# VectorE's instruction order in the two Strassen feed-forward stages of a 1024-token, 22-matrix kernel

## The chip, the cores and the metric

One Trainium2 chip, one of its cores. The metric is device microseconds (us) of one execution of the whole kernel, lower is better. PE is TensorE, DVE is VectorE, ACT is ScalarE, POOL is GpSimd, SP is SyncE (it issues the loads).

## What is computed

Two blocks over a sequence of 1024 tokens, width 1024: two layers of mixed attention, and then one macaron block, which has a SwiGLU feed-forward before and after its mixer. The change touches the feed-forwards alone, which the reference has as

```python
def _swiglu(h, w_gu, w_down):
    g, u = jnp.split(h @ w_gu, 2, axis=-1)
    return (jax.nn.silu(g) * u) @ w_down

    for l in range(DEPTH_2):
        x = x + FFN_RES * _swiglu(_rmsnorm(x, norm_ffn1[l]), w_ffn1_gu[l], w_ffn1_down[l])
        ...
        x = x + FFN_RES * _swiglu(_rmsnorm(x, norm_ffn2[l]), w_ffn2_gu[l], w_ffn2_down[l])
```

with h 1024 x 1024, w_gu 1024 x 5632 (g and u 2816 columns each, 22 tiles of 128) and w_down 2816 x 1024. The root of the mean square is a factor per token: the kernel multiplies by the gain first, starts the matmuls on that, and puts the root (ROOT) on their results.

## The kernel before, in words

**Exact products from halves.** Every float32 operand is cut into a float16 part hi and a bfloat16 part lo, and one product is three matmuls (L1182 to L1184: hi*hi, hi*lo, lo*hi) of 128x128 by 128x512. hi is a copy to float16 by ACT and a clip to the largest float16 by DVE in place; lo = source - hi comes from POOL or from DVE.

**Where an order is written.** Each engine has its own program, written out by hand: the five programs run side by side, each strictly in its own order, and meet at semaphores alone. An instruction that waits holds up all that stands behind it on its engine. Nothing is scheduled by a planner.

**A feed-forward, `ffn(idx)`, idx 1 and 2** (they have the same code on each engine):

1. DVE adds seven tiles of squares (`add_squares`, into `stats`), PE sums them over the partitions, DVE scales that (`variance`, L2180, and with it gives back the accumulator that PE needs for the tile after it), ACT makes the reciprocal root, and `refine` does one Newton step (ROOT in `stats`).
2. The first PLAIN_F = 4 pairs of tiles of g and u are computed plainly, two pairs at a time in the four PSUM tiles. DVE's `plain_pair(f)` takes g times ROOT, lets ACT make the silu, takes u, multiplies by ROOT and cuts the result into its halves.
3. The other 18 pairs (`BLOCKS`) go by a Strassen-like scheme (Winograd's, 7 products in place of 8). The activation is cut into quarters Q11, Q12, Q21, Q22 (each 128 x 2048 in the tensor `residual`). Four differences of quarters are made in place by `term_sum`, each after the one before it; ACT copies T1, T3, T2 and T4 to float16 (`term_part`), DVE clips them, and DVE (T1, T3: `term_split`) or POOL (T2, T4: `term_rest`, L1071) makes the low halves. ACT's order is: silu of pair 0, first weight part, T1, T3, T2, silu of pair 1, weight parts.
4. The weights of a block come as one load of 1 MB (`panel_raw` or `ffn_extra`, by turns, issued when POOL is through with the block before). DVE makes four sums of quarters (`weight_sum(b, 0..3)`, in a chain), ACT makes seven float16 copies, DVE clips them (`weight_clip(b, 0..6)`), and POOL makes the seven low halves (`weight_rest`, L1066).
5. PE's `block(b)` then runs seven products of 12 matmuls each into four accumulators. Between them stand waits; those that matter here are

```python
                        if i == 3:
                            pe.wait_ge(evicted, 9 * n + 1)
                        if i == 5:
                            pe.wait_ge(evicted, 9 * n + 3)
```

   The fourth product (i = 3) waits for DVE's first eviction of the block, `evict(b, 0)`: U2 = second accumulator + the copy of the first, since it writes over the second accumulator. The sixth (i = 5) waits for evictions 1 and 2. `evict(b, 0)` itself waits for the second product and for ACT's copy of the first accumulator (`first_copy`), and in block 0 that copy waits for POOL's T4 (`term_ready_pool`), whose source it writes over.
6. `keep_block(b - 1)`: evictions 6, 7 and 8 of the block before, times ROOT, and its halves. DVE does this when the last product of block b - 1 is done, while PE runs products 1 to 3 of block b.

DVE's loop over the blocks before the change was, in each turn: `keep_block(b - 1)`, the four `weight_sum(b + 1, n)`, `evict(b, 0)`, three weight clips, `evict(b, 1)` and `evict(b, 2)`, two clips, `evict` 3 to 5, two clips. The helper `tt` (L2156) records every tensor_tensor of DVE, so one line stands for many kinds of work; the tensor names tell them apart.

Of the kernel before, what the change touches and what calls it, by code (L numbers as in the profile page):

```python
# [28 lines left out]
ALU = mybir.AluOpType  # L29
# [19 lines left out]
PLAIN_F = 4  # L49
# [336 lines left out]
def build(nc, io):  # L386
    ctx = ExitStack()
    with ctx:
# [84 lines left out]
        B_T1, B_T2, B_T3 = [parts(22528 + 2048 * c, 2048) for c in range(3)]  # L473
# [4 lines left out]
        Q11, Q12, Q21, Q22 = (X4[:, k:k + 4, c:c + HALF] for k in (0, 4) for c in (0, HALF))  # L478
# [120 lines left out]
        normed = sem("operand_normed")  # L599
# [1542 lines left out]
        def _(dve):  # L2142
# [12 lines left out]
            def tt(out, a, b, op):  # L2155
                return V_.tensor_tensor(out, a, b, op)  # L2156
# [21 lines left out]
            def variance(v, section, turn, t, n, eps):  # L2178

                V_.tensor_scalar(v, ready(section, turn, t)[:, :], 1.0 / n, eps, ALU.mult, ALU.add)\  # L2180
                  .then_inc(tile_taken[t % 4], 1)
# [162 lines left out]
            def add_squares(idx):  # L2344

                for k in range(1, KT):
                    dve.wait_ge(square_made, 8 * (idx - 1) + k + 1)
                    tt(SQSUM, SQT[0] if k == 1 else SQSUM, SQT[k], ALU.add).then_inc(square_added, 1)
                    dve.wait_ge(square_added, 7 * (idx - 1) + k)
# [207 lines left out]

            def ffn(idx):
                add_squares(idx)
                variance(SILP[0], f"rms{idx}", 0, 3, D, 1e-6)  # L2560
                refine(SILP[0], ROOT, AFP[0], 3 * LAYERS + 1 + (17 if idx == 2 else 0) + (idx == 2))
                restart()

                def plain_pair(f):
# [7 lines left out]
                    chained(tt(AFP[j], AFP[j], ROOT, ALU.mult))  # L2572
                    t = slice(f * T, (f + 1) * T)
                    split(AP_[0][:, t], AP_[1][:, t], AFP[j], act_split)

                def term_sum(out, a, b, n, after):
                    dve.wait_ge(normed, 12 * (idx - 1) + after)
                    tt(out, a, b, ALU.subtract).then_inc(normed, 1)

                def term_clip(home, n):  # L2580
                    dve.wait_ge(term_hi, 4 * (idx - 1) + n)
                    return V_.tensor_scalar(home[0], home[0], HI_MAX, -HI_MAX, ALU.min, ALU.max)

                def term_split(home, q, n):
                    hi, lo = [v.rearrange("p (k t) -> p k t", k=4) for v in home]
                    chained(term_clip(home, n))
                    tt(lo, q, hi, ALU.subtract).then_inc(term_ready, 1)

                def weight_sum(b, n):
                    a11, a12, a21, a22 = raw_block(b)  # L2590
                    s1, s2, s4 = sums_of(b)
                    g = block_of(idx, b)
                    if n == 0:
                        dve.wait_ge(raw_loaded[b % 2], 16 * ((BLOCKS - b % 2 + 1) // 2 * (idx - 1) + b // 2 + 1))
                        if b > 0:
                            dve.wait_ge(weight_lo, 7 * (g - 1) + 6)
                    out, x, y, op = ((s1, a21, a22, ALU.add), (s2, s1, a11, ALU.subtract), (a21, a11, a21, ALU.subtract),
                                     (s4, a12, s2, ALU.subtract))[n]
                    tt(out, x, y, op).then_inc(sum_made, 1)
                    if n in (0, 1):  # L2600
                        dve.wait_ge(sum_made, 4 * g + n + 1)
# [48 lines left out]
                    split(AP_[0][:, t], AP_[1][:, t], FACT, act_split)  # L2650

                plain_pair(0)
                term_sum(Q11, Q12, Q11, 9, 8)
                term_sum(Q12, Q22, Q12, 10, 9)
                term_sum(Q22, Q22, Q11, 11, 10)
                term_sum(Q21, Q21, Q22, 12, 11)
                plain_pair(1)
                for n in range(4):
                    weight_sum(0, n)
                term_split(B_T1, Q11, 1)  # L2660
                term_clip(B_T2, 3).then_inc(term_clipped, 1)
                term_split(B_T3, Q12, 2)
                for i in range(5):
                    weight_clip(0, i)
                for f in range(2, PLAIN_F):
                    plain_pair(f)
                for i in range(5, 7):
                    weight_clip(0, i)
                term_clip(B_T4, 4).then_inc(term_clipped, 1)
                for b in range(BLOCKS):  # L2670
                    more = b + 1 < BLOCKS
                    if b > 0:
                        keep_block(b - 1)
                    if more:
                        for n in range(4):
                            weight_sum(b + 1, n)
                    evict(b, 0)
                    if more:
                        weight_clip(b + 1, 0)
                        weight_clip(b + 1, 1)  # L2680
                        weight_clip(b + 1, 2)
                    evict(b, 1)
                    evict(b, 2)
                    if more:
                        weight_clip(b + 1, 3)
                        weight_clip(b + 1, 4)
                    for step in (3, 4, 5):
                        evict(b, step)
                    if more:
                        weight_clip(b + 1, 5)  # L2690
                        weight_clip(b + 1, 6)
# [438 lines left out]
```

## Time and profile before

| | |
|---|---|
| time, median of 3 runs | 3399.25 us (3399.2 to 3400.58) |
| the profiled execution | 3400.38 us, of which the span from first to last instruction is 3398.6 us |
| busy: PE, DVE, POOL, ACT | 3241.8 us (95%), 1831.8 (54%), 1611.1 (47%), 1131.2 (33%) |
| chain of waits that ended last | PE 83%, DVE 11%, issue 3%, ACT 2%, POOL 1% |
| granted TensorE clock, mean | 0.989 |
| first product of block 0 on PE | starts at 1227.41 us in the first, at 2807.17 us in the second feed-forward |

Busy time of PE counts the pipelined length of its matmuls, so a short wait hardly lowers it; waits are better read from the view of waits and from the timeline. The chain gives, for each moment, the engine that the end hung on. A row of a timeline is: start in us from the span's start, duration in us, engine, line, operation, out<-in, shapes, count, and in brackets the idle time of the engine before it with what ended it.

### The profile page before, as it was taken

Reading aid. Unit: us, or ns where it says so; the run is one execution under the profiler, and the core shown is the slowest. Engines: PE = TensorE matmul, PEld = TensorE weight load, DVE = VectorE, ACT = ScalarE, POOL = GpSimd, SP = SyncE. Lnnn points to the kernel's source line nnn. Section 1 sums busy time; section 2 is a strip of 40 time slices with the busy share of each in tenths; the row PEclk is TensorE's granted clock in tenths of the full one; section 3 lists DMA queues with packets and bytes.
Section 4 is the critical chain, followed back from the end, with each engine's and each line's share of the span. In section 5 each row is a group of like instructions: output and inputs, shape, how many; then the busy total and the mean of one; then the engine's idle time right before and its main releaser. Section 6 shows DMA issues by size and latency. Waiting matters only on the chain.

```text
span 3398.6 us, 47704 instructions
## 1 busy us (share of the span) xinstructions
PE 3241.8 (95%) x18771; PEld 1657.2 (49%) x19068; DVE 1831.8 (54%) x3065; ACT 1131.2 (33%) x2104; POOL 1611.1 (47%) x1100
## 2 busy tenths in 40 slices
PE   8999998999999879999999999999999998999999
PEld 4555653655654334444445554555554443444444
DVE  4365558146547876664113366666666687676200
ACT  1434422234332522221002445555554432222000
POOL 4555752455664244443333566655664434444332
PEclk9999999999999989999999999999999998999999
DMA  3122112112121211112222011111112211111212
GB/s 131 40 51 62 58 56 101 38 50 65 38 80 39 88 49 51 61 50 96 70 70 90 29 58 52 50 51 52 51 36 93 84 63 50 50 62 38 103 50 83
DMA packets 59276, 211.71 MB, mean 62 GB/s; under 512 B 7344, under 2 KB 7728, under 8 KB 58544
## 3 DMA queue, kind: packets, MB, share of 16 engines
q1 hardware_dynamic: 54304, 191.34, 17.3%
q10 hardware_dynamic: 4752, 17.30, 1.3%
q8 instruction: 154, 2.52, 0.3%
q14 instruction: 66, 0.54, 0.1%
HBM read 181.36 MB, written 20.97 MB: 60 GB/s over the span
## 4 chain that ended last, share of the span: by engine, by line
PE 83%; DVE 11%; issue 3%; ACT 2%; POOL 1%; DMA 0%; DVEq 0%; SPq 0%; POOLq 0%; ACTq 0%
PE pair L1184 24%; PE pair L1182 23%; PE pair L1183 21%; DVE residual L2156 5%; PE pair L1402 3%; PE pair L1371 3%; DVE arena L2156 3%; PE pair L1383 2%; PE pair L1620 1%; PE pair L1646 1%; PE pair L1631 1%; DVE arena L2167 1%; PE pair L1574 1%; PE pair L1202 1%; DVE pair L2156 1%
## 5 line engine op out<-in xcount | busy, mean ns | idle before, releaser
L1182 PE MATMUL pair<-operand,panel_parts 128*128 128x512 f16 x1808 | 691.4, 382 | 42.0 <-DVE operand L2156 26.2
L1184 PE MATMUL pair<-operand,panel_parts 128*128 128x512 f16 x1808 | 689.0, 381 | 8.5
L966 POOL TENSOR_SCALAR panel_parts<-panel_raw 128x1024 f16<-128x1024 f32 (+3 forms) x204 | 208.7, 1023 | 918.7 <-issue 645.0
L1183 PE MATMUL pair<-operand,panel_parts 128*128 128x512 bf16 x1648 | 628.6, 381 | 0.0
L1182 PE MATMUL pair<-arena,panel_parts 128*128 128x512 f16 (+1 forms) x1248 | 470.5, 377 | 16.3 <-DVE residual L2156 7.5
L967 POOL TENSOR_TENSOR panel_parts<-panel_raw,panel_parts 128x1024 bf16<-128x1024 f32 (+3 forms) x204 | 472.6, 2317 | 17.0
L1184 PE MATMUL pair<-arena,panel_parts 128*128 128x512 f16 (+1 forms) x1248 | 469.5, 376 | 4.6
L1003 POOL TENSOR_SCALAR arena<-arena,row_inv 128x256 f32<-128x256 f32 (+7 forms) x256 | 347.5, 1370 | 237.7 <-DVE row_inv L2222 237.5
L1183 PE MATMUL pair<-arena,panel_parts 128*128 128x512 bf16 (+2 forms) x1160 | 436.3, 376 | 0.0
L1182 PEld LDWEIGHTS pair<-operand,panel_parts 128*128 128x128 f16 x1808 | 177.5, 98 | 275.7 <-issue 94.8
L2159 DVE SCALAR_TENSOR_TENSOR residual<-pair,residual 128x1024 f32<-128x1024 f32 (+1 forms) x64 | 61.3, 958 | 420.9 <-PE pair L1184 392.4
L1184 PEld LDWEIGHTS pair<-operand,panel_parts 128*128 128x128 bf16 x1808 | 177.6, 98 | 216.3 <-issue 5.0
L1137 POOL TENSOR_SCALAR arena<-arena,row_inv 128x384 f32<-128x384 f32 (+1 forms) x128 | 192.0, 1511 | 157.8 <-DVE row_inv L2839 157.8
L1183 PEld LDWEIGHTS pair<-operand,panel_parts 128*128 128x128 f16 x1808 | 177.8, 98 | 177.9 <-issue 8.8
L1833 ACT ACTIVATE arena<-arena,neg_max 128x256 f32<-128x256 f32 (+7 forms) x256 | 156.0, 611 | 322.1 <-DVE neg_max L2203 321.6
L2203 DVE CUSTOM_DVE_ANT_0 arena<-pair,arena 128x256 f32<-128x256 f32 (+7 forms) x256 | 133.8, 559 | 146.5 <-PE pair L1371 79.7
L2156 DVE TENSOR_TENSOR arena<-arena 128x1024 f32<-128x1024 f32 (+3 forms) x143 | 195.8, 1369 | 22.3 <-ACT arena L2063 10.6
L1182 PEld LDWEIGHTS pair<-arena,panel_parts 128*128 128x128 f16 x1248 | 121.8, 98 | 175.2 <-issue 41.1
L1184 PEld LDWEIGHTS pair<-arena,panel_parts 128*128 128x128 bf16 x1248 | 122.0, 98 | 144.1 <-issue 0.3
L1183 PEld LDWEIGHTS pair<-arena,panel_parts 128*128 128x128 f16 x1248 | 122.1, 98 | 131.5 <-issue 3.5
L2156 DVE TENSOR_TENSOR residual<-pair,residual 128x512 f32<-128x512 f32 (+1 forms) x168 | 116.8, 713 | 125.8 <-PE pair L1184 124.4
L1735 ACT ACTIVATE arena<-pair 128x512 f32<-128x512 f32 (+2 forms) x210 | 99.4, 504 | 156.8 <-PE pair L1184 128.5
(300 smaller groups left out, 5797.2 us busy)
## 6 DMA issues: line engine op xcount, KB each, us to landing
panel_raw<-in_wl SPq DMA_DIRECT2D x58, 512.0 KB, 3.5
panel_raw<-in_wm SPq DMA_DIRECT2D x56, 512.0 KB, 3.6
ffn_extra<-in_wgu SPq DMA_DIRECT2D x18, 1024.0 KB, 5.0
panel_raw<-in_wgu SPq DMA_DIRECT2D x18, 1024.0 KB, 5.2
panel_raw<-in_wdn SPq DMA_DIRECT2D x32, 512.0 KB, 3.5
residual<-residual_spill SPq DMA_DIRECT2D x31, 512.0 KB, 6.4
residual_spill<-residual ACTq DMA_DIRECT2D x24, 512.0 KB, 2.6
panel_raw<-in_wgu SPq DMA_DIRECT2D x16, 512.0 KB, 3.7
```

The costliest lines, as they stand in the source:

```text
L966: chained(nc.gpsimd.tensor_scalar(hi[:, c], RAW[:, s, c], HI_MAX, -HI_MAX, ALU.min, ALU.max))
L967: nc.gpsimd.tensor_tensor(lo[:, c], RAW[:, s, c], hi[:, c], ALU.subtract).then_inc(panel_split[s], 1)
L1003: nc.gpsimd.tensor_scalar(p, p, RI[:, b:b + 1], None, ALU.mult).then_inc(slot_scaled, 1)
L1137: nc.gpsimd.tensor_scalar(p, p, RI[:, b:b + 1], None, ALU.mult).then_inc(mix_scaled, 1)
L1182: nc.tensor.matmul(out, stat[0], mov[0], start=first, stop=False, skip_group_check=skip)
L1183: nc.tensor.matmul(out, stat[0], mov[1], start=False, stop=False, skip_group_check=skip)
L1184: return nc.tensor.matmul(out, stat[1], mov[0], start=False, stop=last, skip_group_check=skip)
L1371: m = nc.tensor.matmul(out[:, c:c + w], q_of(s, u), k_of(s, u)[:, c:c + w], start=True, stop=True)
L1402: m = nc.tensor.matmul(OUTL[u.h * HD:(u.h + 1) * HD, (i // 2) * P:(i // 2 + 1) * P], v_of(s, u, kt), PTL[g][:, c0:c0 + P], start=j == 0, s ...
L1833: nc.scalar.activation(p, p, ACT.Exp, bias=NM[:, b:b + 1], scale=-1.0, accum_out=RS[:, b:b + 1]).then_inc(slot_probs, 1)
L2156: return V_.tensor_tensor(out, a, b, op)
L2203: m = V_.tensor_tensor_reduce(out=probs_of(n, s, u), in0=score_cols(s, u), in1=bias_of(s, u), scale=-1.0, scalar=3e38, op0=ALU.add, op1=AL ...
```

## The change

Only DVE's program is touched, in both feed-forwards:

- two of the four differences of quarters (Q11 and Q12) are moved from behind `plain_pair(0)` to ahead of `variance`;
- the clip of T2 is put ahead of the cut of T1; the cut of T3 is moved from ahead of the five weight clips and `plain_pair(2)` to between `plain_pair(2)` and `plain_pair(3)`;
- in the loop over the blocks `evict(b, 0)` is put ahead of the four weight sums of the next block.

No instruction is added or taken away, and none changes its shape.

```diff
@@ -2557,6 +2557,12 @@
             def ffn(idx):
                 add_squares(idx)
+                def term_sum(out, a, b, n, after):
+                    dve.wait_ge(normed, 12 * (idx - 1) + after)
+                    tt(out, a, b, ALU.subtract).then_inc(normed, 1)
+
+                term_sum(Q11, Q12, Q11, 9, 8)
+                term_sum(Q12, Q22, Q12, 10, 9)
                 variance(SILP[0], f"rms{idx}", 0, 3, D, 1e-6)
@@ -2650,20 +2652,18 @@
                 plain_pair(0)
-                term_sum(Q11, Q12, Q11, 9, 8)
-                term_sum(Q12, Q22, Q12, 10, 9)
                 term_sum(Q22, Q22, Q11, 11, 10)
                 term_sum(Q21, Q21, Q22, 12, 11)
                 plain_pair(1)
                 for n in range(4):
                     weight_sum(0, n)
+                term_clip(B_T2, 3).then_inc(term_clipped, 1)
                 term_split(B_T1, Q11, 1)
-                term_clip(B_T2, 3).then_inc(term_clipped, 1)
-                term_split(B_T3, Q12, 2)
                 for i in range(5):
                     weight_clip(0, i)
-                for f in range(2, PLAIN_F):
-                    plain_pair(f)
+                plain_pair(2)
+                term_split(B_T3, Q12, 2)
+                plain_pair(3)
                 for i in range(5, 7):
                     weight_clip(0, i)
@@ -2671,11 +2671,10 @@
                     if b > 0:
                         keep_block(b - 1)
+                    evict(b, 0)
                     if more:
                         for n in range(4):
                             weight_sum(b + 1, n)
-                    evict(b, 0)
-                    if more:
                         weight_clip(b + 1, 0)
```

On VectorE, at the start of a feed-forward: the seven adds of squares, the scaling L2180 that PE and ACT wait for, and the first Newton instruction. Of the difference between the two orders:

```order
 L2156 TENSOR_TENSOR stats<-stats,arena 128x1024 x4
 L2156 TENSOR_TENSOR stats<-stats,ffn_extra 128x1024 x2
+L2156 TENSOR_TENSOR residual<-residual 128x4x512 x2
 L2180 TENSOR_SCALAR arena<-pair 128x1024
 L2156 TENSOR_TENSOR arena<-stats 128x1024
```

Two of the differences of quarters (`residual<-residual`) now stand ahead of L2180; the other two stay behind the first plain pair.

On VectorE, where block 0 begins, before the change: the two clips of weight parts 5 and 6, the clip of T4 (`operand<-operand`), the four weight sums of block 1, and then `evict(0, 0)` (`residual<-pair,residual`):

```order
L2606 TENSOR_SCALAR panel_parts<-panel_parts 128x512 x2
L2582 TENSOR_SCALAR operand<-operand 128x2048
L2156 TENSOR_TENSOR arena<-panel_raw 128x512
L2156 TENSOR_TENSOR arena<-arena,panel_raw 128x512
L2156 TENSOR_TENSOR panel_raw<-panel_raw 128x512
L2156 TENSOR_TENSOR arena<-panel_raw,arena 128x512
L2156 TENSOR_TENSOR residual<-pair,residual 128x512
```

and with it:

```order
L2608 TENSOR_SCALAR panel_parts<-panel_parts 128x512 x2
L2584 TENSOR_SCALAR operand<-operand 128x2048
L2156 TENSOR_TENSOR residual<-pair,residual 128x512
L2156 TENSOR_TENSOR arena<-panel_raw 128x512
L2156 TENSOR_TENSOR arena<-arena,panel_raw 128x512
L2156 TENSOR_TENSOR panel_raw<-panel_raw 128x512
L2156 TENSOR_TENSOR arena<-panel_raw,arena 128x512
```

The eviction has gone past four sums; the same exchange stands in every later block but the last, behind `keep_block`.

## Rows read from the trace of the kernel before

**Rows 1.** View of waits, first feed-forward (1120 to 1640 us): total, times, longest
```profile
PE pair L1182 <- DVE residual L2156: 25.1, 17, 10.0
PE pair L1182 <- DVE arena L2156: 5.8, 1, 5.8
```
**Rows 2.** View of waits, second feed-forward (2700 to 3230 us)
```profile
PE pair L1182 <- DVE residual L2156: 24.8, 17, 9.7
```
**Rows 3.** Timeline of PE, end of third and start of fourth product of one block
```profile
1363.74 0.38 PE L1184 MATMUL pair<-arena,panel_parts 128*128 128x512 f16 x1
1365.07 0.38 PE L1182 MATMUL pair<-arena,panel_parts 128*128 128x512 f16 x1 [0.94 <-DVE residual L2156]
1365.28 0.38 PE L1183 MATMUL pair<-arena,panel_parts 128*128 128x512 bf16 x1
```
**Rows 4.** Timeline of DVE, same block: first sum, evict 0, three clips, evict 1
```profile
1361.58 0.68 DVE L2156 TENSOR_TENSOR residual<-panel_raw 128x512 f32<-128x512 f32 x1
...
1364.23 0.68 DVE L2156 TENSOR_TENSOR residual<-pair,residual 128x512 f32<-128x512 f32 x1
1364.84 0.69 DVE L2606 TENSOR_SCALAR residual<-residual 128x512 f16<-128x512 f16 x3
1367.85 0.69 DVE L2156 TENSOR_TENSOR residual<-pair,residual 128x512 f32<-128x512 f32 x1 [2.33 <-PE pair L1184]
```
**Rows 5.** Timelines of ACT (first copy) and POOL (first low half), same block
```profile
1358.98 0.60 ACT L1735 ACTIVATE residual<-pair 128x512 f32<-128x512 f32 x1 [3.09 <-PE pair L1184]
...
1365.20 1.34 POOL L1066 TENSOR_TENSOR residual<-panel_raw,residual 128x512 bf16<-128x512 f32 x1 [7.42 <-DVE residual L2606]
```
**Rows 6.** Timelines of DVE and POOL around the first feed-forward's root
```profile
1163.29 1.22 DVE L2156 TENSOR_TENSOR stats<-stats,ffn_extra 128x1024 f32<-128x1024 f32 x1
1168.31 1.23 DVE L2180 TENSOR_SCALAR arena<-pair 128x1024 f32<-128x1024 f32 x1 [3.79 <-PE pair L1202]
1188.63 2.29 DVE L2156 TENSOR_TENSOR residual<-residual 128x2048 f32<-128x2048 f32 x1
1190.96 3.01 DVE L2156 TENSOR_TENSOR residual<-residual 128x2048 f32<-128x2048 f32 x1
...
1166.67 1.04 POOL L966 TENSOR_SCALAR panel_parts<-panel_raw 128x1024 f16<-128x1024 f32 x1 [5.75 <-PE pair L1184]
```
**Rows 7.** Timelines of ACT and DVE: first weight part, and pair 1's u
```profile
1192.65 0.63 ACT L1735 ACTIVATE ffn_extra<-ffn_extra 128x512 f16<-128x512 f32 x1 [15.80 <-DMA ffn_extra<-in_wgu]
...
1200.08 1.22 DVE L2156 TENSOR_TENSOR arena<-pair,arena 128x1024 f32<-128x1024 f32 x1 [4.98 <-ACT arena L1924]
```
**Rows 8.** Timelines where block 0 begins: DVE first sum and evict 0, POOL T4, ACT copy
```profile
1239.22 1.63 DVE L2156 TENSOR_TENSOR arena<-panel_raw 128x512 f32<-128x512 f32 x1
...
1246.56 0.69 DVE L2156 TENSOR_TENSOR residual<-pair,residual 128x512 f32<-128x512 f32 x1
...
1240.27 4.50 POOL L1071 TENSOR_TENSOR operand<-residual,operand 128x2048 bf16<-128x2048 f32 x1
...
1244.88 0.60 ACT L1735 ACTIVATE residual<-pair 128x512 f32<-128x512 f32 x1 [9.30 <-POOL operand L1071]
```
**Rows 9.** Windows: us, busy of PE, PEld, DVE, ACT, POOL, granted clock, DMA share, GB/s
```profile
1241.00:1252.00 11.00, 4.61 (x11) 1.65 (x12) 6.81 (x7) 3.19 (x6) 7.32 (x4) 0.54 0.28 95
```
**Rows 10.** Timelines of DVE and POOL around the second feed-forward's root
```profile
2742.32 1.22 DVE L2156 TENSOR_TENSOR stats<-stats,ffn_extra 128x1024 f32<-128x1024 f32 x1
2748.07 1.22 DVE L2180 TENSOR_SCALAR arena<-pair 128x1024 f32<-128x1024 f32 x1 [4.52 <-PE pair L1202]
...
2746.43 1.04 POOL L966 TENSOR_SCALAR panel_parts<-panel_raw 128x1024 f16<-128x1024 f32 x1 [5.22 <-PE pair L1184]
2747.55 2.12 POOL L967 TENSOR_TENSOR panel_parts<-panel_raw,panel_parts 128x1024 bf16<-128x1024 f32 x1
...
2762.17 4.05 POOL L967 TENSOR_TENSOR panel_parts<-panel_raw,panel_parts 128x1024 bf16<-128x1024 f32 x1
```
**Rows 11.** Timeline of DVE, the five weight clips of block 0
```profile
1219.73 3.98 DVE L2606 TENSOR_SCALAR ffn_extra<-ffn_extra 128x512 f16<-128x512 f16 x5
```

More of the change, by code:

```diff
@@ L2574, in plain_pair @@
                     split(AP_[0][:, t], AP_[1][:, t], AFP[j], act_split)
-                def term_sum(out, a, b, n, after):
-                    dve.wait_ge(normed, 12 * (idx - 1) + after)
-                    tt(out, a, b, ALU.subtract).then_inc(normed, 1)
                 def term_clip(home, n):
```

## The prediction, made before the change was run

> **What bounds the kernel now.** The page comes first: PE is busy for 95% of the span and the chain runs through it for 83%, but 11% of the chain is DVE. So there are places where PE stands and DVE is what it stands for. The view of waits of the two feed-forwards names them. In the first, PE's L1182 waited 17 times for DVE's `residual`, 25.1 us, the longest 10.0, and once for `arena`, 5.8 us [rows 1]; in the second it is the same, 24.8 and 9.7 [rows 2]. The longest is block 0. The other 16 make 15.1 us, 0.94 each, and they are blocks 1 to 16 (block 17 has no next block, so no sums stand ahead of its eviction).
>
> The timeline of one such block shows what is behind it. The last matmul of product 3 starts at 1363.74, the first of product 4 at 1365.07, 1.33 us later, where matmuls otherwise follow at 0.21 [rows 3]. So the stall is 1.12 us (the idle time in the row is less, since a matmul's row is longer than its pitch). PE was released by evict 0, which ran from 1364.23 to 1364.91. Ahead of it on DVE stood the four weight sums, from 1361.58 [rows 4]. Their results are wanted for the next block. ACT's copy of the first accumulator, the other thing evict 0 needs, was there at 1359.58 [rows 5].
>
> **Part 1, evict 0 ahead of the sums (blocks 1 to 16).** It can start where the first sum did, at 1361.58. The second product is done by then: with product 4 due at 1363.95 (1363.74 + 0.21) and 12 matmuls of 0.215 to a product, product 3 began at 1361.4, and a matmul's row ends 0.17 after the next one's start. Evict 0 ends at 1362.26 and PE is released 0.16 later, as it was before (1364.91 to 1365.07). Product 4 is due at 1363.95, so 1.5 us are left and the stall goes wholly: 16 x 1.12 x 2 = 35.8 us.
>
> What is late next? The sums start 0.7 later, but evict 0 no longer stands between them and the clips, so the first clip stays at 1364.84 and POOL at 1365.20 [rows 4, 5]. ACT's copies of the sums come 0.7 later and are off the path: these weights are wanted a whole block later. Evict 1 may start 1.12 earlier, at 1366.73, and DVE is through with the three clips at 1365.53. Evicts 1 and 2 take 1.4 and must end before product 6, due at 1363.95 + 2 x 2.58 = 1369.1; that gives evict 1 until 1367.5, 2.0 us after DVE is free. All later evictions hang on PE's products. The next load of weights waits for POOL's low halves, which keep their place against PE. DVE has room: it was idle for 2.33 us before evict 1 alone [rows 4], and a block of 84 matmuls takes PE 18.1 us in place of 19.2. Cost beside the gain: nothing, while those 2.0 us hold.
>
> **Part 2, evict(0, 0).** It gains less than its place suggests. It needs ACT's first copy, which waited for POOL's T4 until 1244.88 [rows 8]. DVE will now stand at the eviction and the sums behind it wait. What goes is the remainder of the sums: the copy ends at 1245.48, evict 0 can start at about 1245.6 instead of 1246.56, 1.0 us. POOL's 4.50 [rows 8] also gets shorter: DVE's first sum, 1.63 where such a sum takes 0.68 [rows 4], ended at 1240.85, after POOL's operation began at 1240.27; if POOL waited for it, 0.5 us more goes. Bounds 1.0 and 1.5; I take 1.5, since the sum's extra length shows that the two do exclude each other. Twice: -3.0 us. Block 1's sums now end at about 1248.4 instead of 1246.7, ten us before their block begins. The granted clock is 0.54 around this start [rows 9], as PE has stood for 10 us, and it will have stood at least as long: no change taken; if the half-rate stretch moved by one or two us it would be worth about 1 us either way.
>
> **Part 3, T2's clip, T3 and the plain pairs.** T3's cut no longer delays `plain_pair(2)`, so product 1 starts some 3 us earlier and the 5.8 us wait [rows 1] shrinks. It is worth nothing: PE then waits the longer before product 4, whose release (part 2) hangs on `plain_pair(3)` and the clips behind it, and ahead of those stands the same work as before. T3 is ready before product 4, since it stands one plain pair ahead. Cover gone: if part 2's wait were not there, this would show.
>
> **Part 4, two differences ahead of the root.** DVE is idle for 3.79 us before L2180 [rows 6]. Free, such a difference takes 2.29, against POOL 3.01 [rows 6]. In the first feed-forward Q11 runs from 1164.55 to 1166.85; then POOL has just begun an operation (1166.67), which is when I take the difference of 3.01 and not that of 2.29, so Q12 ends at 1169.88. L2180 starts at 1169.8 instead of 1168.31: 1.5 us late, and with it PE's next tile, the panels that follow on POOL, and the weight load behind them on SP's queue. That load releases ACT at 1192.65 [rows 7], ACT makes three copies and pair 1's silu, and DVE waits 4.98 us for that at 1200.08 [rows 7]. So all 1.5 us arrive, and what the two sums leave free behind plain pair 0 falls into that idle time: +1.5.
>
> In the second feed-forward the adds end at 2743.54 and Q12 would run from 2745.9 to 2748.2. POOL's operation comes at 2746.43 [rows 10], after Q12's start. If Q12 is then undisturbed, L2180 starts at 2748.1 instead of 2748.07, no delay; with the 3.01 of the other row it would be 0.8 late. I take none, since the difference at 1188.63 [rows 6] took its 2.29 with the next operations of both engines close behind it. The Trainium skill ("SBUF — State Buffer", section "Who interferes with whom") says that whichever of the two starts first holds the shared port for its whole instruction and the other blocks; by it this term is 0.0, by the contended row alone +0.8. POOL's second operation then falls on `refine` (some 0.8 us on DVE alone, not on PE). At 2762.17 POOL's low half took 4.05 where a free one takes 2.12 [rows 10], for it stood behind a difference; with two of them gone and DVE's order shifted by 0.8 it waits less, and the weight load goes out earlier by between 0 and 1.9. I take 1.4: DVE's cut of pair 0 then still costs POOL part of it. It comes through the same chain as above: -1.4.
>
> **Sum.** -35.8 - 3.0 + 1.5 - 1.4 = -38.7. The profiled execution took 3400.38 (span 3398.6), which gives 3361.7. It lies 1.1 above the median of the runs, 3399.25, so the expected median is **3361**, between the two (1.1% faster). Changes below 0.2%, 6.8 us, cannot be told from none here.
>
> **The rivals.**
>
> *POOL holds DVE up and the stall comes back at product 6 (slower).* The place: the sums and three clips between evict 0 and evict 1. Five such clips took 3.98 us against POOL, where three take 0.69 free [rows 11, 4], and a sum took 1.63 in place of 0.68 [rows 8, 4]. If all were contended, DVE would be free at 1364.84 + 4 x 0.95 + 3 x 1.25 = 1372.4 and evict 1 start 4.9 us after its latest moment of 1367.5. Each block then loses 4.9 and wins 1.12: 32 x 3.8 = +121, less the 2.9 of the other parts, 3518. With the clips alone it is 1.1, and nothing changes: about 3396. It decides from 1368.8 on: 1.3 too late makes it slower by over 0.2%. Against it: POOL was idle for 7.42 us until 1365.20 [rows 5], as it is fed by these very clips. The same page's rule, that the second to issue waits for the whole instruction, would give these numbers if POOL were at work there; the trace has it idle. 2 in 100.
>
> *Another releaser.* The releaser is inferred from semaphores; if product 4 hung on a weight part or T term too, the change would do nothing: 3396 to 3402. Against it: the stall is the same 1.12 in sixteen blocks, 0.16 after evict 0. 3 in 100.
>
> *Half a gain.* Evict 0 stands at its inputs' very moment; if something on DVE or ACT then moves the later evictions so that about half the stall returns at product 5 or 6: -18 in place of -35.8, 3379. For it speaks only that the new loop has never run at 18.1 us a block. 7 in 100.
>
> *The root comes later than I take.* If all four moved differences take 3.01, L2180 is 2.3 late in the first (1164.55 + 6.05 = 1170.6) and 1.5 late in the second feed-forward, and the 1.4 is not won: +3.8 in place of +0.1, 3364. If PE's next tile then also begins at half rate, some 2 us more each, 3368. 10 in 100 for both.
>
> The forecast itself: 78 in 100. Its own bounds: part 2 and 4 reach from -2.0 + 1.5 + 0.8 = +0.3 to -3.0 + 0.7 - 1.9 = -4.2 (Q12 of the first undisturbed), and 2 us for the clock, so 3358 to 3366. The range takes in the late root and part of the half gain at the top: 3356 to 3372, which leaves about 15 in 100 out. Faster by over 0.2%: 0.95; within 0.2%: 0.03; slower: 0.02.
>
> **What would show it.** Right: in the view of waits PE's waits for `residual` fall from 17 to 1 in each feed-forward, fourth products follow third ones at 0.21 us, and blocks repeat at 18.1 instead of 19.2 us. DVE's evict 0 directly follows `keep_block`. The wait before product 1 drops to 2 to 4 us, the one before product 4 of block 0 grows and stays ended by DVE's `residual`. L2180 comes 1.5 us later after its adds in the first feed-forward and at the same time in the second. Wrong: any repeated wait of PE at product 5 or 6, a POOL operation between evict 0 and evict 1, or a block period over 18.3 us.

## The result, and the profile after

The changed kernel takes 3362.02 us (median of 4 runs, 3360.74 to 3364.86) against 3399.68 (3399.2 to 3400.58, 4 runs): a ratio of 0.989, 95% interval 0.9873 to 0.9907. The profiled execution took 3360.86, with a span of 3359.1. The prediction was 3361, from 3356 to 3372.

The page's part on the chain, where DVE had 11% before:

```profile
PE 90%; DVE 5%; issue 2%; ACT 2%; POOL 1%; DMA 1%; DVEq 0%; SPq 0%; ACTq 0%; POOLq 0%
```

The view of waits of the changed kernel, first feed-forward (1120 to 1640 us), answers to [rows 1]:

```profile
PE pair L1182 <- DVE residual L2156: 11.8, 1, 11.8
PE pair L1182 <- DVE arena L2156: 3.1, 1, 3.1
```

and the second (2700 to 3230 us) to [rows 2]:

```profile
PE pair L1182 <- DVE residual L2156: 13.5, 1, 13.5
PE pair L1182 <- DVE arena L2156: 1.5, 1, 1.5
```

Seventeen waits for `residual` have become one in each, block 0's. That one has grown. Counted from the end of the adds of squares, product 1 starts 0.3 us later than before in the first feed-forward and product 4 1.7 later; in the second they start 4.3 and 2.9 earlier. The timeline of PE at one of the later blocks, where product 4 begins:

```profile
1359.65 0.38 PE L1184 MATMUL pair<-arena,panel_parts 128*128 128x512 f16 x1
1359.87 0.38 PE L1182 MATMUL pair<-arena,panel_parts 128*128 128x512 f16 x1
```

The 1.33 us of [rows 3] are 0.22. The timeline of DVE in the same block, from evict 0 over the first sum and the three clips to evict 1, answers to [rows 4]:

```profile
1357.55 0.69 DVE L2156 TENSOR_TENSOR residual<-pair,residual 128x512 f32<-128x512 f32 x1
1358.16 0.68 DVE L2156 TENSOR_TENSOR residual<-panel_raw 128x512 f32<-128x512 f32 x1
...
1360.81 1.67 DVE L2608 TENSOR_SCALAR residual<-residual 128x512 f16<-128x512 f16 x3
1362.66 0.69 DVE L2156 TENSOR_TENSOR residual<-pair,residual 128x512 f32<-128x512 f32 x1 [0.18 <-PE pair L1184]
```

Evict 0 ends at 1358.24 and product 4 starts at 1359.87 without waiting. The three clips take 1.67 where they took 0.69, as the third of them now waits for POOL's low half (POOL's timeline):

```profile
1361.17 1.15 POOL L1066 TENSOR_TENSOR residual<-panel_raw,residual 128x512 bf16<-128x512 f32 x1 [7.49 <-DVE residual L2608]
```

The same low half took 1.34 before and delayed no clip [rows 4, 5]. That holds for every block that has a next one: before, POOL's operation took the longer time in all 34 places, and with the change the clip took it, 1.26 in place of 0.28, in 31 of 34.

All 17 steps from block to block, taken at each block's evict 3, are 18.13 us in both feed-forwards; before, 16 of them were 19.23.

**Where the 39.5 us of span went.** Each stretch between two marks of DVE's timeline, in the two profiled executions:

| stretch | before | after | difference | predicted |
|---|---|---|---|---|
| start to end of the first adds of squares | 1164.52 | 1164.78 | +0.3 | 0 |
| first feed-forward: to evict(0, 0) | 82.04 | 83.71 | +1.7 | 0.0 |
| to evict 3 of block 0 | 8.49 | 7.98 | -0.5 | 0 |
| to evict 3 of block 17 | 325.85 | 308.21 | -17.6 | -17.9 |
| to the end of the second adds of squares | 1162.65 | 1161.04 | -1.6 | 0 |
| second feed-forward: to evict(0, 0) | 82.77 | 79.86 | -2.9 | -2.9 |
| to evict 3 of block 0 | 8.79 | 7.68 | -1.1 | 0 |
| to evict 3 of block 17 | 325.86 | 308.21 | -17.7 | -17.9 |
| to the end | 237.61 | 237.60 | 0.0 | 0 |

The blocks carry 35.3 of it. What the first feed-forward lost ahead of block 0 (1.7) and what came back in three stretches that were forecast unchanged (0.5, 1.6, 1.1) is mostly TensorE's clock and the two early differences, which the next rows show. From evict(0, 0) to evict 3 of block 0 the granted clock was 0.68 before and 0.72 after in the first feed-forward, and 0.65 and 0.75 in the second.

**The start of the first feed-forward.** Timelines of DVE, and of POOL, at the root of the changed kernel, to be read against [rows 6]:

```profile
1164.81 5.33 DVE L2156 TENSOR_TENSOR residual<-residual 128x2048 f32<-128x2048 f32 x2
1170.07 1.21 DVE L2180 TENSOR_SCALAR arena<-pair 128x1024 f32<-128x1024 f32 x1
...
1183.57 2.71 POOL L966 TENSOR_SCALAR panel_parts<-panel_raw 128x1024 f16<-128x1024 f32 x1 [11.44 <-issue]
```

The two differences took 5.33 (2.29 and 3.01), and L2180 came 5.29 after the adds where it came 3.79 after them: 1.5 late, as forecast. But PE, released by it, then ran at about half rate. Windows of 1170 to 1174 us (columns as in [rows 9]), first before, then after:

```profile
1170.00:1174.00 4.00, 4.00 (x20) 1.83 (x19) 3.28 (x3) 1.90 (x2) 0.00 (x0) 1.00 0.45 131
```

```profile
1170.00:1174.00 4.00, 2.66 (x7) 1.01 (x8) 2.84 (x4) 2.34 (x2) 2.13 (x1) 0.63 0.17 39
```

The granted clock was 1.00 after an idle PE of about 1.4 us, and 0.63 now, after 2.9 us: part of these 4 us went at the lower of its two levels, 1.2 GHz in place of 2.4. From 1171.34 to 1174.30 matmuls follow at 0.43 us instead of 0.215, which makes PE's tile end 1.5 us later still. POOL's next operation, which began 15.8 us after the adds before, began at 18.8, took 2.71 in place of 2.01 as it met a remaining difference, and its second half (4.05 in both) ended 3.7 us later. The weight load behind it released ACT at

```profile
1196.67 0.63 ACT L1735 ACTIVATE ffn_extra<-ffn_extra 128x512 f16<-128x512 f32 x1 [18.07 <-DMA ffn_extra<-in_wgu]
```

31.9 us after the adds, against 28.1 [rows 7].

The lower clock does not follow from the idle time alone. Seven of the traced kernels have the early differences in the first feed-forward, and in all of them L2180 comes 5.29 us after the adds and PE idles for 2.9 us. In four (this one, the old order of T1 to T3, the relaxed wait and the turned-round start) PE restarts at the lower level. In three (the rest without evict 0, three sums ahead, two operations more) it restarts at full clock, and ACT is released 29.6 to 29.7 us after the adds, which is 1.5 us late and no more. The window of the kernel with two operations more, whose adds end within 0.01 us of the same place:

```profile
1170.00:1174.00 4.00, 2.65 (x13) 1.24 (x14) 2.84 (x4) 2.34 (x2) 2.15 (x1) 1.00 0.21 34
```

**The second feed-forward** went as worked out: POOL's operation came after the second difference had begun and was the one to wait, 2.67 in place of 1.04 [rows 10], and L2180 was not delayed. Timelines of DVE and POOL:

```profile
2725.76 4.62 DVE L2156 TENSOR_TENSOR residual<-residual 128x2048 f32<-128x2048 f32 x2
2730.29 1.22 DVE L2180 TENSOR_SCALAR arena<-pair 128x1024 f32<-128x1024 f32 x1
...
2728.60 2.67 POOL L966 TENSOR_SCALAR panel_parts<-panel_raw 128x1024 f16<-128x1024 f32 x1 [5.22 <-PE pair L1184]
2743.84 2.98 POOL L967 TENSOR_TENSOR panel_parts<-panel_raw,panel_parts 128x1024 bf16<-128x1024 f32 x1
```

POOL's low half took 2.98 in place of the 4.05 of [rows 10], and evict(0, 0) came 2.91 us earlier.

**Block 0.** Timelines of POOL, ACT and DVE, against [rows 8]:

```profile
1243.70 4.05 POOL L1071 TENSOR_TENSOR operand<-residual,operand 128x2048 bf16<-128x2048 f32 x1
...
1247.86 0.60 ACT L1735 ACTIVATE residual<-pair 128x512 f32<-128x512 f32 x1 [8.85 <-POOL operand L1071]
...
1248.49 0.69 DVE L2156 TENSOR_TENSOR residual<-pair,residual 128x512 f32<-128x512 f32 x1 [5.76 <-ACT residual L1735]
```

DVE stands at the eviction for 5.76 us, and POOL's T4 takes 4.05 instead of 4.50 as no sum is in its way.

**Between the feed-forwards** nothing was changed, yet 1.6 us went. There is a stretch at the end of the mixer where PE has stood and restarts at half rate; it was longer in the profiled execution before than in the one after. Eight of the twelve traces have 1162.6 to 1162.7 us for the whole stretch, so the 1161.04 of this one is the exception, and the gain of 1.6 belongs to the execution, not to the change. Windows, before and after:

```profile
2702.00:2710.00 8.00, 6.49 (x17) 2.36 (x18) 6.72 (x5) 4.41 (x5) 4.82 (x3) 0.57 0.85 316
```

```profile
2686.00:2694.00 8.00, 6.72 (x25) 2.73 (x26) 6.52 (x6) 4.18 (x5) 4.60 (x3) 0.79 0.87 320
```

### The profile page after: what moved, and what is told of

Read it like the earlier page. It is cut to its first block, busy times and chain, and to the rows that moved or that the text cites. A ratio compares the mean times of both kernels' runs of the same rounds, so it can differ in the third digit from the quotient of the medians.

```text
span 3359.1 us, 47704 instructions
## 1 busy us (share of the span) xinstructions
PE 3231.6 (96%) x18771; PEld 1658.5 (49%) x19068; DVE 1871.2 (56%) x3065; ACT 1130.5 (34%) x2104; POOL 1596.1 (48%) x1100
## 4 chain that ended last, share of the span: by engine, by line
PE 90%; DVE 5%; issue 2%; ACT 2%; POOL 1%; DMA 1%; DVEq 0%; SPq 0%; ACTq 0%; POOLq 0%
PE pair L1184 26%; PE pair L1182 26%; PE pair L1183 23%; PE pair L1402 3%; PE pair L1371 3%; PE pair L1383 2%; DVE arena L2156 2%; PE pair L1620 1%; PE pair L1646 1%; PE pair L1631 1%; PE pair L1574 1%; DVE stats L2156 1%; PE pair L1202 1%; DVE residual L2156 1%; PE pair L1360 0%
```

## The experiments

Every kernel was timed against the kernel before on the same chip; the kernel before had a median of 3398.86 beside the runs of evict 0 alone, the rest without it, the early differences taken back and the old order of T1 to T3; of 3399.48 beside the next four; and of 3400.68 beside the two with early differences in the second feed-forward only. Theory A is the prediction's: the repeated stall is the sums ahead of evict 0, and all else is small. Its rivals say that the start moves share in the gain, or that something else releases PE.

The stretch ahead of the first feed-forward took 1159.8 to 1166.6 us in the twelve traces, with the same code in all of them. So where a difference of a few us matters, the length of each feed-forward in the traces is given too, from the end of its adds of squares to evict 3 of block 17: 416.4 and 417.4 us before, 399.9 and 395.8 with the whole change.

### Evict 0 alone

The kernel before, with only this edit:

```diff
                         keep_block(b - 1)
+                    evict(b, 0)
                     if more:
                         for n in range(4):
                             weight_sum(b + 1, n)
-                    evict(b, 0)
```

> The kernel before with one edit: evict(b, 0) ahead of the four weight sums; sums, clips and splits at the start stay where they were. If the sums ahead of the eviction are the whole of the repeated stall, blocks repeat at 18.13 us and 32 x 1.10 = 35.2 us go, and evict(0, 0) gains its 1.5 us in each feed-forward too (3.0), so about 3361 to 3362, the same as the whole change within 2 us. Rival: the gain needs the earlier differences and splits as well (for instance because the first blocks would start late and stay late); then a good part is missing, 3375 or more, or the block period lies above 18.13.

3362.48 us (3361.15 to 3363.25), ratio 0.9893 (0.9876 to 0.9909). All 17 block steps are 18.13 us, and evict(0, 0) comes 80.5 us after the adds in the first feed-forward (before 82.0) and 81.0 in the second (82.8). The feed-forwards take 397.6 and 397.6 us, together 0.5 less than with the whole change. One exchange carries the whole gain.

### The rest without it

The whole change, with evict 0 put back behind the sums.

> The whole change with evict(b, 0) put back behind the four weight sums; the two early differences and the new order of clips and splits stay. If they are worth what the two traces suggest (the first feed-forward 1.7 us later, the second 1.4 us earlier), the time is within 3 us of 3399.7, and blocks repeat at 19.23 us. Rival: the start is where part of the 38 us came from: 3392 or less.

3400.5 us (3392.57 to 3403.61, 10 runs), ratio 1.0005 (0.9995 to 1.0015): no difference. The view of waits of its first feed-forward has the seventeen waits again:

```profile
PE pair L1182 <- DVE residual L2156: 30.0, 17, 15.0
```

Its profiled execution happened to be its fastest, 3392.57; 4.6 of its 7.8 us less had gone before the first feed-forward began, where the programs are the same. A single execution of it can't be used for a few us.

### The early differences taken back

```diff
                 add_squares(idx)
-                term_sum(Q11, Q12, Q11, 9, 8)
-                term_sum(Q12, Q22, Q12, 10, 9)
                 variance(SILP[0], f"rms{idx}", 0, 3, D, 1e-6)
...
                 plain_pair(0)
+                term_sum(Q11, Q12, Q11, 9, 8)
+                term_sum(Q12, Q22, Q12, 10, 9)
                 term_sum(Q22, Q22, Q11, 11, 10)
```

> The whole change with the two differences of quarters put back behind the first plain pair. In the first feed-forward L2180 follows the end of the adds by 3.8 us again and no longer by 5.3, PE's next tile does not fall to half rate, and evict(0, 0) comes 1.7 to 3 us earlier against the end of the adds; in the second L2180 stays at 4.5 us and evict(0, 0) comes 1.4 later. Together 0 to -2 us against the whole change: 3359 to 3363. Rival: the early differences pay in both, because they use DVE's idle time: then 3364 or more.

3361.48 us (3361.22 to 3363.67). Evict(0, 0) comes 80.5 us after the adds in the first feed-forward, where the whole change has 83.7, and 81.0 in the second, where it has 79.9. So in these traces the early differences cost 3.2 us in the one and win 1.2 in the other; over the whole feed-forwards (397.7 and 397.7) it is 2.2 and 1.9, and the times show no difference clear of the noise. The granted clock at PE's restart is full again (window of 1169 to 1174 us):

```profile
1169.00:1174.00 5.00, 4.96 (x23) 2.27 (x24) 3.69 (x4) 2.34 (x2) 0.36 (x1) 1.00 0.36 105
```

### Early differences in the second feed-forward only

```diff
                 add_squares(idx)
-                term_sum(Q11, Q12, Q11, 9, 8)
-                term_sum(Q12, Q22, Q12, 10, 9)
+                if idx == 2:
+                    term_sum(Q11, Q12, Q11, 9, 8)
+                    term_sum(Q12, Q22, Q12, 10, 9)
```

(and behind plain pair 0 for idx 1).

> The whole change, with the two early differences in the second feed-forward only; in the first they stand behind plain pair 0 as before. Against the end of the adds evict(0, 0) came 83.7 us later with them in the first and 80.5 without, and 79.9 with and 81.0 without in the second. So each is at its better value: about 3 us less than the whole change, 3358 to 3361. Rival: the difference in the first feed-forward is the clock's doing in one execution and averages out: 3361 to 3363.

3359.78 us (3358.02 to 3361.49), beside 3400.68 for the kernel before. Evict(0, 0) comes 80.5 and 79.6 us after the adds, the better value in each. The ranges of this kernel and of the whole change touch, so as a time the 2 to 3 us are likely and not settled. The feed-forwards of its trace take 397.7 and 395.3, together 2.7 less than those of the whole change.

### The old order of T1, T2 and T3

The whole change with

```diff
-                term_clip(B_T2, 3).then_inc(term_clipped, 1)
                 term_split(B_T1, Q11, 1)
+                term_clip(B_T2, 3).then_inc(term_clipped, 1)
+                term_split(B_T3, Q12, 2)
                 for i in range(5):
                     weight_clip(0, i)
                 plain_pair(2)
-                term_split(B_T3, Q12, 2)
                 plain_pair(3)
```

> The whole change with the old order of T1, T2 and T3 (T3's cut ahead of the five weight clips and the third plain pair). PE's wait before product 1 of block 0 grows by about 3 us in each feed-forward (3.5 to 6.4 between starts in the first, 1.8 to 4.8 in the second) and its wait before product 4 shrinks by as much; the time stays within 2 us of 3362. Rival: the 3 us arrive at the end, twice: 3368.

3362.76 us (3360.93 to 3365.34). In the first feed-forward's waits, PE's before product 1 is 6.2 us instead of 3.1, and the one before product 4 is 8.2 instead of 11.8:

```profile
PE pair L1182 <- DVE residual L2156: 8.2, 1, 8.2
PE pair L1182 <- DVE arena L2156: 6.2, 1, 6.2
```

The earlier third plain pair is paid back in full one wait later, as the prediction's part 3 has it.

### How much slack evict 0 has

The whole change, with evict 0 behind three of the four sums.

```diff
-                    evict(b, 0)
                     if more:
-                        for n in range(4):
+                        for n in range(3):
                             weight_sum(b + 1, n)
+                    evict(b, 0)
+                    if more:
+                        weight_sum(b + 1, 3)
```

> The whole change, but evict(b, 0) stands behind three of the four weight sums instead of ahead of all. In the changed kernel it ends 1.5 us before product 4 is due; three sums take 2.05 us. If that slack is real, 0.55 to 0.6 us per block come back, blocks repeat at 18.7 us, and 32 of them make +18, about 3380. Rival: the stall hangs on something else that the move happened to relieve (POOL's or ACT's order), then the period stays 18.13, or goes to 19.23 at once.

3375.6 us (3375.5 to 3375.78), ratio 0.9928 (0.9912 to 0.9945). The block steps are 18.63 us, so 0.50 came back in each of 32 blocks. The timeline of PE where product 4 starts, and of DVE with evict 0 between the third and the fourth sum:

```profile
1284.88 0.38 PE L1184 MATMUL pair<-arena,ffn_extra 128*128 128x512 f16 x1
1285.60 0.38 PE L1182 MATMUL pair<-arena,ffn_extra 128*128 128x512 f16 x1 [0.34 <-DVE residual L2156]
```

```profile
1284.77 0.68 DVE L2156 TENSOR_TENSOR residual<-pair,residual 128x512 f32<-128x512 f32 x1
1285.37 0.68 DVE L2156 TENSOR_TENSOR arena<-panel_raw,arena 128x512 f32<-128x512 f32 x1
```

PE starts 0.15 us after evict 0's end, at whatever place the end is, so the release is evict 0, and nothing else: the rival of another releaser is out. The time came out 4 us below the expected 3380; 2 of them are in the 32 blocks, which gave back 15.9 in place of 18.

### POOL's work between evict 0 and evict 1

The whole change, with two operations more per block. Their results go nowhere.

```diff
                         weight_clip(b + 1, 2)
+                        for _ in range(2):
+                            tt(STAT[:, _ * HALF:(_ + 1) * HALF], ROOT[:, 0:HALF], ROOT[:, HALF:T], ALU.add)
                     evict(b, 1)
```

> The whole change with two operations more on VectorE in each block, between the three weight clips and evict(b, 1): sums of two halves of ROOT into the unused first quarter of stats, 128x512, both inputs in SBUF, as a weight sum; 0.69 us each when free. The output does not depend on them. In the changed kernel evict 1 starts at 1362.66 and product 6 would be held from 1363.46 on; DVE is free at 1362.48. If POOL, which works there, holds each of them up for one of its 1.16 us operations, evict 1 starts near 1365.7, 2.2 late, and 32 blocks give +70, about 3433. If POOL and VectorE do not exclude each other, it starts at 1363.8, 0.3 late, +10, about 3372. If product 6 does not hang on evict 1 and 2 at all, 3362.

3422.67 us (3420.61 to 3427.99), ratio 1.0071 (1.0054 to 1.0088): 61 us more than the whole change, for 2 x 0.69 us of work in each of 34 places. The timeline of DVE in one block, and the one of POOL over the same time:

```profile
1291.00 3.20 DVE L2156 TENSOR_TENSOR stats<-stats 128x512 f32<-128x512 f32 x2
1294.13 0.68 DVE L2156 TENSOR_TENSOR residual<-pair,residual 128x512 f32<-128x512 f32 x1
```

```profile
1290.90 2.76 POOL L1066 TENSOR_TENSOR residual<-arena,residual 128x512 bf16<-128x512 f32 x2
```

The two sums take 3.20 in place of 1.4, 1.64 each: POOL and DVE go by turns. Product 6 then waits for evict 2, 17 times, 25.2 us in all:

```profile
PE pair L1182 <- DVE pair L2156: 25.2, 17, 1.9
```

The block steps are 19.18 or 20.16 us, so a block loses 1.05 or 2.03, where 2.2 were expected; 24 of the 34 steps are of the longer kind, 8 of the shorter, and two lose 0.04 or less. So the rival that would have made the change slower is a real mechanism, and the price was of the right size. What kept it away is that the changed kernel has only the third clip in POOL's way. With two operations more there, the loss is larger than what the change had won.

### The wait of block 0's first copy

The quarter that ACT's copy writes over is Q12, and evict 0 writes over a part of Q22; POOL's T4 reads Q21, which evict 1 is the first to write over. So the wait of the first copy for T4 does not protect the source of T4, as the description of the kernel before has it: the copy never touches that quarter.

```diff
                     if b == 0:
                         act.wait_ge(term_ready, 2 * idx)
-                        act.wait_ge(term_ready_pool, 2 * idx)
+                        act.wait_ge(term_ready_pool, 2 * idx - 1)
...
                     elif step == 1:
                         dve.wait_ge(product_done, 7 * g + 4)
+                        if b == 0:
+                            dve.wait_ge(term_ready_pool, 2 * idx)
```

> The whole change, where ACT's copy of the first accumulator of block 0 waits for T1, T2 and T3 alone, and evict(0, 1), which writes over Q21, waits for POOL's T4 instead. If POOL's T4 is what holds block 0's fourth product, evict(0, 0) follows T4's clip directly, some 5.8 us earlier in each feed-forward (6.0 instead of about 11.8 us idle before product 4), of which product 6 gives back 1 to 3, as evict(0, 1) then comes behind sums that wait for POOL: 3350 to 3356. Rival: block 0 is held by its chain on VectorE (plain pair 3 and the clips), and POOL's T4 lies in its shadow: 3360 or more.

3354.66 us (3350.08 to 3360.96), ratio 0.9862 (0.9846 to 0.9879). PE's wait before product 4 is 5.9 us in place of 11.8, and a new one of 3.0 stands before product 6, whose evictions come behind sums that POOL holds up:

```profile
PE pair L1182 <- DVE residual L2156: 5.9, 1, 5.9
PE pair L1182 <- DVE arena L2156: 3.0, 1, 3.0
PE pair L1182 <- DVE pair L2156: 3.0, 1, 3.0
```

So POOL's T4 did hold block 0, and half or more of what its removal frees is given back behind it: the feed-forwards take 398.3 and 392.1 us, 1.6 and 3.6 less than with the whole change. Its executions lie 11 us apart and the profiled one is the slowest: in it the stretches that the edit does not touch were 5.1 us longer than in the trace of the whole change. So the 7 us between the medians are uncertain by some us, and the traces show 5.

### Block 0 turned round

The relaxed wait, and T4, the first copy and evictions 0 to 2 of block 0 moved forward. DVE's part is below. On ACT T4's copy and the first copy go ahead of plain pair 3's silu, and on POOL T4 ahead of the low halves of weights 5 and 6. The loop then leaves out evictions 0 to 2 of block 0.

```diff
                 term_split(B_T3, Q12, 2)
+                term_clip(B_T4, 4).then_inc(term_clipped, 1)
+                evict(0, 0)
                 plain_pair(3)
                 for i in range(5, 7):
                     weight_clip(0, i)
-                term_clip(B_T4, 4).then_inc(term_clipped, 1)
+                evict(0, 1)
+                evict(0, 2)
```

> As the run with the relaxed wait, and in block 0 the order is turned round on three engines: T4 is copied, clipped and cut ahead of plain pair 3 (on POOL ahead of the low halves of weights 5 and 6), the first copy and evict(0, 0) stand ahead of plain pair 3 too, and evicts 1 and 2 of block 0 ahead of block 1's sums. Then product 4 follows product 3 without a wait, product 6 waits for evict 2 behind plain pair 3 (about 1244.4 in the first feed-forward), and product 7 starts at about 1247 where it starts at 1258.6 now: 10 to 12 us in each feed-forward, 3338 to 3345. Rival: the work on VectorE is the same, so block 0's end hangs on its sum and the wait only moves to product 6, 7 or the first product of block 1: 3352 or more.

3341.43 us (3341.13 to 3348.93), ratio 0.9835 (0.9819 to 0.9852). Product 4 follows product 3 without a wait. What PE still waits for from 1150 to 1300 us is product 1, the root, block 1's fourth product and product 6, in the order of the lines:

```profile
PE pair L1184 <- DVE arena L2160: 3.0, 1, 3.0
PE pair L1184 <- DVE arena L2184: 2.9, 1, 2.9
PE pair L1184 <- DVE residual L2160: 2.7, 1, 2.7
PE pair L1184 <- DVE pair L2160: 1.7, 1, 1.7
```

(The added lines move the helpers' numbers: L2160 is `tt`, L2184 the scaling.) This kernel has the lowest median of the study, 20.6 us under the whole change, and is by 1.65% faster than the kernel before. Its feed-forwards take 392.1 and 386.7 us, 7.8 and 9.1 less than with the whole change and not 10 to 12; the other 3.3 us of the difference between the two traced spans lie in stretches that the edit does not touch.

### Both together

The turned-round start, with early differences in the second feed-forward only.

> The turned-round start of block 0 (the run called hoisted) together with early differences in the second feed-forward only. The first plain tiles and the weight load come some 1.5 to 3 us earlier in the first feed-forward, and with block 0 now close behind them that arrives at the end: 3337 to 3341 against 3341.4. Rival: block 0 now hangs on the time at which PE ends the plain tiles and not on the load; then 1 us or less is gained.

3342.88 us (3341.85 to 3344.98), ratio 0.9832 (0.9818 to 0.9845). As a time it is not faster than the one before it, and the expected gain is missed. The traces show why this does not speak for the rival. Evict(0, 0) comes 67.1 us after the first adds in place of 70.1, and the first feed-forward takes 389.0 us in place of 392.1, so the 3.1 us do arrive at its end; the second takes 387.1 in place of 386.7. But the stretch ahead of the first feed-forward, which has the same code, took 1165.26 us in this profiled execution and 1159.82 in the other. A gain of 3 us is lost among such differences between executions.

## Why the prediction was right

**Part 1, the sums ahead of evict 0: right.** 32 x 1.12 = 35.8 was forecast and 35.3 measured (17.64 and 17.65 between evictions 3 of blocks 0 and 17); the edit alone gives the whole gain. The slack of 1.5 us was right: evict 0 ended 1.63 before product 4 started, 0.15 of which is the release, and three sums ahead brought back 0.50. **The slack of evict 1 was half of what I wrote.** The prediction left the three clips at 0.69 and had 2.0 us. POOL's low half caught the third clip (1.67), DVE was free at 1362.48 and evict 1 had until about 1363.46. It cost nothing, but two operations more took the rest, as their run shows. A sign of being wrong was badly chosen here: "a POOL operation between evict 0 and evict 1" occurs with the change (1361.17), and it stood there before it as well (1365.20, between 1364.23 and 1367.85 [rows 4, 5]), so it could not tell anything.

**Part 2, evict(0, 0): right.** 1.5 us in each feed-forward were forecast; with evict 0 alone it came 1.5 earlier after the adds in the first and 1.8 in the second. Of the two bounds the upper was the right one, since POOL's T4 went from 4.50 to 4.05.

**Part 3, T3 and the plain pairs: right.** The old order gives the same time with the waits shared out otherwise; product 1 starts 3.2 us later with it in the first feed-forward and 2.6 in the second. The wait before product 1 was forecast at 2 to 4 us and is 3.1 in the first and 1.5 in the second.

**Part 4, the early differences: right in the second, mis-sized in the first.** Forecast +1.5 and -1.4, measured up to evict(0, 0) by the trace without them +3.2 and -1.2. The 1.5 us by which L2180 is late was exact. The step that failed is that all behind it was taken to keep its distance: PE, idle for 2.9 us in place of 1.4, restarted at the lower clock, its tile took 1.5 us longer, and POOL's panel met a difference at another point. Where the clock stayed up, the forecast holds: with two operations more, whose program is the same up to that point, evict(0, 0) comes 82.0 us after the adds, 1.5 later than the 80.5 without early differences. So the term is 1.5 or about 3.2, as the clock falls, and the prediction had the clock only in a rival, for both feed-forwards; it fell in the first alone.

**The total was right also by luck.** 1.7 too few in the first feed-forward's start were made up by shorter stretches at half rate elsewhere (0.5, 1.1 and the 1.6 in the mixer), which no step forecast. The changed kernel's own executions differ by 4 us, and those of the change without evict 0 by 11.

**A size in a rival.** The bound of 1.3 us, from which the rival of POOL makes the kernel slower by 0.2%, leaves out the 2.9 us of the other parts; with them it is 1.4.

The Trainium skill's rule ("SBUF — State Buffer", section "Who interferes with whom"), that the later of VectorE and GpSimd waits for the other's whole instruction, was the one to go by. By it Q12 in the second feed-forward would run free, and it did (4.62 for two). It also fits the two added operations at 1.64 each, between POOL operations of 1.16 free. Of the 1.64 some 0.95 are the wait. What the rule does not give is who comes first when both are ready at the same moment: the third clip is recorded 0.04 us after POOL's low half before the change and with it, and the clip waits in none of the 34 places before and in 31 of them with it.

The rival of half a gain and the one of another releaser did not occur: no wait repeats, and PE's release follows evict 0 wherever it is put.

## What to carry to other kernels

In a hand-written order, put the instruction that the busiest engine waits for ahead of work that is only wanted a stage later, and first look up in the trace that its other inputs are there at that moment; the gain is the stall, not the length of what it overtakes. Then work out the slack of the next release too, with the shared port counted in: here 1 us was left, and two operations more of 0.69 us each turned the gain into a loss. Work moved into an engine's idle time ahead of a release is free only if it ends in time: it was 1.5 us late, and cost 1.5 us where the waiting engine's clock held and 3.2 where it fell.

## What was not expected of the hardware

After an idle PE of 2.9 us, before one and the same tile, the granted clock was at its lower level for some 3 us in four traces (0.63 from 1170 to 1174 us in the changed kernel) and at full level in three. After 1.4 us it was at full level in all 17 places, five in first and twelve in second feed-forwards. Ahead of the idle time the two that are shown side by side look alike: PE busy for all of 1155 to 1164 us at a granted clock of 1.00, in the changed kernel and in the one with two operations more. What decides between the two was not found.

Nor do the start times tell which of POOL and VectorE has to wait when they meet: the third clip of a block was recorded 0.04 us after POOL's operation in both kernels (1365.24 after 1365.20 before, 1361.21 after 1361.17 with the change). Before, the clip took 0.29 and POOL's operation 1.34; with the change they took 1.26 and 1.15.
